# Convolution taps in turn over four channel blocks, and 89 of them beside the projections, in a hybrid encoder step on Trainium2

## The chip, the cores and the metric

One NeuronCore of one Trainium2 chip runs the whole layer as one program. The metric is the device time of that core in microseconds: the median of three runs, 654.04 us for the kernel before (653.13 to 656.37). Everything is float32 at the interface; there is one launch.

## The reference

One inference step of a one-layer streaming encoder over 528 prompt frames (16 learned meta tokens and 512 frames) and 32 sample frames of a running stream. Cut to what matters here:

```python
h = rmsnorm(x, g_mix)
proj = h @ w_in                                   # 1024 -> 2560
a_val, a_gate, q, k, v = jnp.split(proj, [512, 1024, 1536, 2048], axis=-1)
u = a_val * jax.nn.sigmoid(a_gate)                # 512 channels
u_hist = jnp.concatenate([conv_hist, u], axis=1)
a_out = jax.nn.silu(layernorm(causal_dwconv(u_hist, conv_w, conv_b), ln_g, ln_b))   # 31 taps per channel
b_out = head_rmsnorm(stick_breaking(q, k_all, v_all, q_start), g_sb)                # 8 heads x 64
x = x + jnp.concatenate([a_out, b_out], axis=-1) @ w_out
x = x + hier_moe(rmsnorm(x, g_ffn), ...)          # 32 experts, 2 per token
```

The depthwise convolution gives `conv[ch, t] = sum over j of w[j, ch] * u[ch, t + j]`, j = 0 to 30, and its result is needed first by the layer norm over channels. Outputs are both streams' final rows and the new keys, values and convolution histories.

## The kernel before

The five engines run their own instruction streams, joined by semaphores. The time falls into these stages: input norm and transposes (to about 50 us), the projections (to 153 us), attention (159 to 282 us), output projection and router (to about 390 us), the experts (to about 620 us) and the final norm.

**Projections.** TensorE computes the first 2048 columns of `w_in` as 16 products of 128 columns each, in the order gate 0, value 0, gate 1, value 1, ... (four channel blocks i), then k and q in four pairs. Each is done as high and low parts in fp32r: 3 x 16 matmuls of 288 columns, 48 in all (line 903). ScalarE rounds each weight tile to its high part (`upper`, line 1366), Pool subtracts it from the tile for the low part (`lower`, line 658: 128 x 1024, two SBUF inputs). `upper(j)` waits until product j - 3 is done. TensorE's product j waits for both parts, and from j = 4 to 11 also for the sigmoid (`sig_done`, even j) and for the gated product (`u_done`, odd j) of the pair four products before, since they share PSUM banks; there are eight banks, two for each product.

**The gated product.** For each channel block i VectorE waits for both projections and the sigmoid, and writes `u = value * sigmoid(gate)` with three instructions (lines 1609 to 1611, a PSUM and an SBUF input each).

**Taps.** The convolution of block i is 31 VectorE instructions over 128 x 590 (both streams with their histories lie side by side): the first is a `tensor_scalar` (line 1593), the others a `scalar_tensor_tensor` (line 1595) that multiplies a shifted slice of `u` with a weight per partition and adds the running `conv[:, i, :]`. `tap` passes each one to `link`, which makes the engine wait for its completion before the next instruction. After block i's last tap two instructions add the bias (line 1599) and give `yc_ready`. The list `taps` goes through block 0's 31 taps, then block 1's, and so on. `TAPS_EARLY = (13, 13, 13, 33)` of them, 72, follow the four gated products; the remaining 52 go into attention's steps, two each (`TAPS_STEP`).

```python
def link(ins):
    chain[0] += 1
    ins.then_inc(dve_chain, 1)
    dve.wait_ge(dve_chain, chain[0])
```

**Into attention.** TensorE transposes eight blocks of cached keys into PSUM (line 950, with a filler matmul at line 956 behind each). ScalarE copies the even ones to SBUF (line 1398), VectorE the odd ones (line 1677), which stand behind the 72nd tap in its program. Transpose n waits from n = 4 on for the copy of n - 4. The first scores wait for all eight copies.

**Attention.** 46 steps: 14 for the sample stream and the prompt's last frames (256 columns for all heads, "few") and 32 for the prompt (one head and one block of 128 keys, 128 to 512 columns, "many"); two few and one many take turns until the few are out at step 20. In step s TensorE makes scores (lines 966, 968 or 979, 982), ScalarE |z|, exp and ln (lines 1417, 1419, 1435), VectorE the softplus (`softplus`, line 1654), Pool the running sum of earlier blocks (lines 701 to 715), TensorE adds it to the scores (`reduce_later`, lines 996 to 1001), ScalarE exponentiates (line 1407) and TensorE weighs the values (`weigh`, lines 1014, 1028). In VectorE's program step s holds the softplus of step s - 1, two taps, and the output copy of a finished unit (lines 1665, 1670). From `LN_STEP = 30` the layer norm goes on between: Pool adds the four `yc` (line 685) in steps 27 to 29, TensorE takes the mean (line 1037) in step 30, VectorE the deviations from step 31.

**Behind attention** come the output projection (line 1098), stores, the router, and the experts, whose weights (2048 KB and 1024 KB for each expert) stream in behind one another. SyncE issues their first loads after the outputs of attention have been stored.

Of the kernel before, what the change touches and what calls it, by code (L numbers as in the profile page):

```python
# [11 lines left out]
ALU = mybir.AluOpType  # L12
# [12 lines left out]
NI = CC // P  # L25
# [8 lines left out]
TAPS = 31  # L34
HIST = TAPS - 1
UW = HIST + TP + HIST + TS
# [7 lines left out]
PAIRS = NE // 2  # L44
RING = 3
HALVED = 2
TAPS_EARLY = (13, 13, 13, 33)
TAPS_STEP = 2
LN_STEP = 30
LAG = 5  # L50
# [7 lines left out]
def build(nc, x_prompt, x_sample, cache_k, cache_v, cache_conv, meta, g_mix, w_in, conv_w, conv_b,  # L58
          ln_g, ln_b, g_sb, w_out, g_ffn, w_rg, b_rg, w_re, b_re, w_ei, w_eo, g_fin,
          y_p, y_s, nk_p, nv_p, ncv_p, nk_s, nv_s, ncv_s):  # L60
    with ExitStack() as ctx:
        def sb(name, shape, dt=F32):
            return ctx.enter_context(nc.sbuf_tensor(name, shape, dt))

        def sem(name):
            return ctx.enter_context(nc.semaphore(name))
# [24 lines left out]
        u = uflat.rearrange("p (i t) -> p i t", i=NI)  # L91
# [10 lines left out]
        cwt = sb("cwt", [P, NI, TAPS])  # L102
# [13 lines left out]
        def part(lo, n):  # L116
            return big[:, lo:lo + n]
# [4 lines left out]
        conv = part(14336, 4 * (UW - HIST)).rearrange("p (i t) -> p i t", i=NI)  # L122
# [123 lines left out]
        dve_chain = sem("dve_chain")  # L246
# [358 lines left out]
        def _(pool):  # L605
# [48 lines left out]
            def lower(j):  # L654

                slot = win[j % WSLOTS]
                pool.wait_ge(w_hi_ready, j + 1)
                pool.tensor_tensor(w_lo[j % WSLOTS], slot, w_hi[j % HSLOTS].bitcast(F32), ALU.subtract).then_inc(w_lo_ready, 1)  # L658
# [1 line left out]
            for j in range(13):  # L660
                lower(j)
            for i in range(NI):

                split = min(13 + 2 * i, 16)
                if i in (1, 2):
                    pool.wait_ge(qpair_ready, 2 * i + 1)
                    for j in range(11 + 2 * i, split):
                        lower(j)
                pool.wait_ge(w_lo_ready, split)
                pool.wait_ge(qk_done, 2 * i + 2)  # L670
                for r in range(2):
                    pool.tensor_copy(qpair[64 * r:64 * r + 64, :, i, 32 * r:32 * r + 32],
                                     qt[64 * r:64 * r + 64, i, 512:COLS].rearrange("p (a t) -> p a t", a=2)).then_inc(qpair_ready, 1)

            pool.wait_ge(z_ready, 1)
            for s, st in enumerate(steps):
# [3 lines left out]
                i = s - LN_STEP + NI  # L680
# [5 lines left out]
                i = s - LN_STEP - 3  # L686
# [842 lines left out]
        def _(dve):  # L1529
            chain = [0]  # L1530
# [5 lines left out]
# [5 lines that stand above are left out]
# [47 lines left out]
            low_part(4)  # L1588


            def tap(i, j):
                if j == 0:
                    link(dve.tensor_scalar(conv[:, i, :], u[:, i, 0:CW], cwt[:, i, 0:1], None, ALU.mult))
                else:
                    link(dve.scalar_tensor_tensor(conv[:, i, :], u[:, i, j:j + CW], cwt[:, i, j:j + 1],  # L1595
                                                  conv[:, i, :], ALU.mult, ALU.add))
                if j == TAPS - 1:
                    for dst, src in ((yc[:, i, 0:TP], conv[:, i, 0:TP]), (yc[:, i, S0:COLS], conv[:, i, US:US + TS])):
                        dve.tensor_scalar(dst, src, vt[:, 8 + i:9 + i], None, ALU.add).then_inc(yc_ready, 1)

            CW = UW - HIST
            taps = [(i, j) for i in range(NI) for j in range(TAPS)]
            dve.wait_ge(small_ready, 3)
            for i in range(NI):
                dve.wait_ge(proj_done, 2 * i + 2)
                dve.wait_ge(sig_done, i + 1)

                b, sg = proj_bank(2 * i + 1), sgm[i % 2]
                dve.tensor_tensor(u[:, i, HIST:HIST + HALF], ps[:, b, 0:HALF], sg[:, 0:HALF], ALU.mult).then_inc(conv_done, 1)
                dve.tensor_tensor(u[:, i, HIST + HALF:HIST + TP], ps[:, b + 1, 0:TP - HALF], sg[:, HALF:TP], ALU.mult).then_inc(conv_done, 1)  # L1610
                dve.tensor_tensor(u[:, i, UW - TS:UW], ps[:, b + 1, S0 - HALF:HALF], sg[:, S0:COLS], ALU.mult).then_inc(u_done, 1)
                dve.wait_ge(conv_done, 2 * i + 2)
                dve.wait_ge(u_done, i + 1)
                for _ in range(TAPS_EARLY[i]):
                    tap(*taps.pop(0))

            def deviation(i):

                if i == 0:
                    dve.wait_ge(mean_done, 1)  # L1620
                    dve.wait_ge(yc_ready, 2 * NI)
                dve.scalar_tensor_tensor(halves(yc[:, i, :]), ps[:, 6:8, 0:HALF], 1.0 / CC,
                                         halves(yc[:, i, :]), ALU.mult, ALU.add).then_inc(dev_ready, 1)

            def variances():
                dve.wait_ge(var_done, 1)
                dve.tensor_scalar(halves(lnv), ps[:, 6:8, 0:HALF], -1.0 / CC, EPS, ALU.mult, ALU.add).then_inc(lnv_ready, 1)

            def refine(j):

                if j == 0:
                    dve.wait_ge(lnr_done, 1)
                    dve.wait_ge(lnv_ready, 1)
                    link(dve.tensor_tensor(lnt, lnr, lnr, ALU.mult))
                elif j == 1:
                    link(dve.tensor_tensor(lnt, lnt, lnv, ALU.mult))
                elif j == 2:
                    link(dve.tensor_scalar(lnt, lnt, -0.5, 1.5, ALU.mult, ALU.add))
                else:
                    link(dve.tensor_tensor(lnr, lnr, lnt, ALU.mult))  # L1640
                    dve.wait_ge(dev_ready, NI)

            def normed(i):
                dve.tensor_tensor(yc[:, i, :], yc[:, i, :], lnr, ALU.mult).then_inc(norm_ready, 1)


            def softplus(s):
                st = steps[s]
                (r0, r1), n = st["rows"], st["n"]
                dve.wait_ge(l_done, s + 1)  # L1650
                if s >= 3:
                    dve.wait_ge(zr_ready, s - 2)
                    dve.wait_ge(cs_ready, sums[s - 3])
                dve.scalar_tensor_tensor(el[s % 3][r0:r1, 0:n], ps[r0:r1, s % 4, 0:n], 0.0, za[s % 3][r0:r1, 0:n],  # L1654
                                         ALU.max, ALU.add).then_inc(el_ready, 1)

            def unit_out(s):
                st = steps[s]
                if not st["last"]:
                    return  # L1660
                dve.wait_ge(av_done, s + 1)
                o = ps[:, unit_bank(st["unit"]), :]
                if "h" in st:
                    h = st["h"]
                    dve.tensor_copy(ot[:, 0:4, 64 * h:64 * h + 64],
                                    o[:, 0:256].rearrange("p (t d) -> p t d", t=4)).then_inc(o_ready, 1)
                else:
                    p0 = st["p0"]
                    for q in range(4):
                        ins = dve.tensor_copy(ot[p0:p0 + 32, 4, :].rearrange("p (a h d) -> p a h d", a=2, h=4)[:, :, q, :],  # L1670
                                              o[32 * q:32 * q + 32, 0:128].rearrange("p (a d) -> p a d", a=2))
                    ins.then_inc(o_ready, 1)
# [6 lines left out]
            for s in range(NS + 4):  # L1679
                if 0 <= s - LN_STEP - 1 < NI:  # L1680
                    deviation(s - LN_STEP - 1)
                if s == LN_STEP + 10:
                    variances()
                if 0 <= s - LN_STEP - 12 < 4:
                    refine(s - LN_STEP - 12)
                if 0 <= s - LN_STEP - 16 < NI:
                    normed(s - LN_STEP - 16)
                if 1 <= s <= NS:
                    softplus(s - 1)
                for _ in range(TAPS_STEP):  # L1690
                    if taps:
                        tap(*taps.pop(0))
                if s >= 4:
                    unit_out(s - 4)

# [2 lines left out]
            for lo, w, cc in ((0, P, slice(0, 4)), (0, 64, slice(4, 5))):  # L1698
# [6 lines left out]
                ins = dve.tensor_tensor(o4, o4, st8.unsqueeze(2).broadcast_to([w, k * HEADS, HD]), ALU.mult)  # L1705
# [289 lines left out]
```

## Time and profile before

| what | before |
|---|---|
| median of 3 runs | 654.04 us (653.13 to 656.37) |
| the profiled execution | 654.35 us, its span 652.6 us |
| mean granted clock of TensorE | 0.937 |
| TensorE (matmul) busy | 557.4 us, 85% of the span |
| VectorE busy | 297.4 us, 46% |
| ScalarE, Pool busy | 165.8 us, 163.0 us |
| DMA | 144.44 MB, mean 221 GB/s; 94% busy from 390 us on |

The span goes from the first to the last instruction; the execution's time has 1.75 us more around it. Matmuls overlap in the records, so TensorE's busy time is an upper reading. Durations of single instructions are in ns or us from start to the acknowledged end; where two of one engine overlap, the start-to-start time is what counts for its throughput. "Idle before" stands in square brackets with what ended it.

### The profile page before, as it was taken

How to read it: one execution, taken by the hardware profiler on the slowest of the kernel's cores; microseconds unless marked ns; L12 is line 12 of the kernel's file. 1: busy time of each engine (PE TensorE's matmuls, PEld its weight loads, DVE VectorE, ACT ScalarE, POOL GpSimd, SP SyncE). 2: the span in 40 equal slices, each digit the busy share in tenths (PEclk: the TensorE clock that was granted, in tenths of full speed). 3: DMA queues.
4: the chain of work that ended last, by engine and by line, in shares of the span. 5: the costliest groups of instructions: out<-in, count | busy, mean ns of one | idle time of the engine just before them, and what ended most of it. 6: DMA issues, size and time to landing. Idle time of an engine off the chain costs nothing.

```text
span 652.6 us, 8215 instructions
## 1 busy us (share of the span) xinstructions
PE 557.4 (85%) x3117; PEld 344.8 (53%) x3118; DVE 297.4 (46%) x483; ACT 165.8 (25%) x321; POOL 163.0 (25%) x215
## 2 busy tenths in 40 slices
PE   3999999999999989988999879999997877879700
PEld 2449999998777566645455473434332322323200
DVE  1531999998789823453415862121120210202037
ACT  2222122213466647732111210101010000000112
POOL 2041534441434444231100330121120210200013
PEclk9999999999599989988999969999998997989955
DMA  8703523105006000002974739999999999999675
GB/s 279 192 1 102 157 74 89 34 1 172 28 3 258 1 0 1 1 5 73 320 302 162 286 108 421 422 424 422 421 426 425 423 426 426 425 418 423 262 273 168
DMA packets 42747, 144.44 MB, mean 221 GB/s; under 512 B 6967, under 2 KB 23375, under 8 KB 34008
## 3 DMA queue, kind: packets, MB, share of 16 engines
q1 hardware_dynamic: 38103, 134.78, 53.1%
q0 software_dynamic: 4608, 9.18, 3.8%
q8 instruction: 22, 0.36, 0.2%
q14 instruction: 14, 0.11, 0.0%
HBM read 136.16 MB, written 15.39 MB: 232 GB/s over the span
## 4 chain that ended last, share of the span: by engine, by line
PE 44%; DVE 22%; DMA 20%; SPq 6%; issue 2%; POOL 2%; ACT 2%; DVEq 0%; POOLq 0%; ACTq 0%
DVE big L1595 16%; DMA low<-in_w_expert_in 11%; PE ps L1257 9%; PE ps L1098 7%; DMA big<-in_w_expert_out 4%; PE ps L874 4%; PE ps L1282 3%; SPq L567 3%; PE ps L1001 3%; SPq L524 2%; PE ps L966 2%; PE ps L903 2%; DMA big<-y_dram 2%; PE ps L1014 1%; PE ps L996 1%
## 5 line engine op out<-in xcount | busy, mean ns | idle before, releaser
L1595 DVE SCALAR_TENSOR_TENSOR big<-low,cwt,big 128x590 f32<-128x590 f32 x120 | 126.8, 1056 | 3.6
L1257 PE MATMUL ps<-big,cw 128*64 128x512 f32 x352 | 79.5, 603 | 12.8 <-DMA big<-in_w_expert_in 6.5
L1909 DVE TENSOR_TENSOR low<-low,ps 128x256 f32<-128x256 f32 x16 | 6.7, 421 | 181.1 <-ACT low L1492 181.1
L903 PE MATMUL ps<-cw_r 128*128 128x288 f32 x256 | 73.0, 295 | 0.0
L903 PE MATMUL ps<-low_r,cw_r 128*128 128x288 f32 x256 | 72.8, 294 | 0.0
L903 PE MATMUL ps<-cw_r,big_r 128*128 128x288 f32 x256 | 72.7, 294 | 0.0
L1257 PEld LDWEIGHTS ps<-big,cw 128*64 128x64 f32 x352 | 28.5, 139 | 62.0 <-issue 62.0
L1098 PE MATMUL ps<-cw,low 128*128 128x512 f32 x128 | 58.1, 610 | 1.7 <-ACT low L1440 1.2
L658 POOL TENSOR_TENSOR big_r<-big,cw_r 128x1024 fp32r<-128x1024 f32 x16 | 40.7, 2547 | 55.1 <-ACT cw_r L1366 55.1
L903 PEld LDWEIGHTS ps<-cw_r 128*128 128x128 f32 x256 | 47.4, 188 | 0.4 <-issue 0.4
L1282 PE MATMUL ps<-big,low 128*64 128x512 f32 x176 | 40.2, 597 | 8.3 <-DVE low L1915 7.3
L903 PEld LDWEIGHTS ps<-cw_r,big_r 128*128 128x128 f32 x256 | 47.2, 188 | 0.0
L903 PEld LDWEIGHTS ps<-low_r,cw_r 128*128 128x128 f32 x256 | 47.2, 187 | 0.0
L1257 PE MATMUL ps<-low 128*64 128x512 f32 x160 | 39.4, 649 | 7.5 <-DMA low<-in_w_expert_in 7.5
L1098 PEld LDWEIGHTS ps<-cw,low 128*128 128x128 f32 x128 | 24.4, 195 | 30.3 <-issue 29.2
L1500 ACT ACTIVATE cw<-ps,low 128x1024 f32<-128x1024 f32 x16 | 17.8, 1114 | 86.4 <-PE ps L1282 86.4
L1492 ACT ACTIVATE low<-ps 128x256 f32<-128x256 f32 x16 | 6.1, 383 | 126.2 <-PE ps L1257 126.2
L1654 DVE SCALAR_TENSOR_TENSOR big<-ps,big 128x256 f32<-128x256 f32 (+4 forms) x46 | 21.5, 470 | 34.2 <-ACT big L1435 29.1
L751 POOL CAST low<-low 128x1 int32<-128x1 f32 (+1 forms) x16 | 3.0, 189 | 130.1 <-PE ps L1241 118.3
L645 POOL TENSOR_TENSOR stat<-stat,nhalf 128x1 f32<-128x1 f32 (+1 forms) x15 | 16.0, 1068 | 78.0 <-DVE stat L1754 39.4
L1001 PE MATMUL ps<-big,negs 128*128 128x256 f32 (+4 forms) x92 | 33.7, 450 | 0.3 <-DVE big L1654 0.3
L1257 PEld LDWEIGHTS ps<-low 128*64 128x64 f32 x160 | 14.2, 151 | 32.1 <-issue 32.1
(247 smaller groups left out, 834.8 us busy)
## 6 DMA issues: line engine op xcount, KB each, us to landing
big<-in_w_expert_in SPq DMA_DIRECT2D x20, 2048.0 KB, 25.5
big<-in_w_expert_out SPq DMA_DIRECT2D x22, 1024.0 KB, 29.1
low<-in_w_expert_in SPq DMA_DIRECT2D x8, 2048.0 KB, 25.8
big<-in_w_in SPq DMA_DIRECT2D x20, 512.0 KB, 5.1
low<-in_w_expert_out SPq DMA_DIRECT2D x10, 1024.0 KB, 32.8
cw<-in_w_out SPq DMA_DIRECT2D x1, 4096.0 KB, 14.1
low<-in_w_expert_in SPq DMA_DIRECT2D x4, 1024.0 KB, 34.4
big<-in_w_expert_in SPq DMA_DIRECT2D x4, 1024.0 KB, 27.8
```

What stands on the lines that cost most here:

```text
L567: sp.dma_start(wi[q][:, ks], w_ei[0, 2 * g + half].rearrange("(p k) n -> p k n", p=P)[:, ks]).then_inc(landed[q], 16)
L645: pool.tensor_tensor(t, t, nhalf[0:t.shape[0], :].broadcast_to(list(t.shape)), ALU.pow).then_inc(rstd_ready, 1)
L658: pool.tensor_tensor(w_lo[j % WSLOTS], slot, w_hi[j % HSLOTS].bitcast(F32), ALU.subtract).then_inc(w_lo_ready, 1)
L874: mm = pe.matmul(ps[0:w, 4 + c % 2, :], ht[:, k, P * c:P * c + w], wv[:, k, :], start=k == 0, stop=k == KD - 1)
L903: return pe.matmul(ps[:, proj_bank(j) + half, 0:HALF], w[:, k, :], h[:, k, cols], start=first, stop=last, skip_group_check=True)
L1001: pe.matmul(z[r0:r1, 0:n], ntri[r0:r1, r0:r1], el[s % 3][r0:r1, 0:n], start=False, stop=True, skip_group_check=True).then_inc(zr_ready, 1)
L1098: mm = pe.matmul(ps[0:w, 4 + 2 * (c % 2) + n, :], mixt[:, k, P * c:P * c + w], wout[:, k, 512 * n:512 * n + 512], start=k == 0, stop=k == ...
L1257: mm = pe.matmul(ps[TILE * half:TILE * half + TILE, GU_BANK[s], :], xt[s][:, k, TILE * half:TILE * half + TILE], wi[2 * s + half][:, k, :] ...
L1282: mm = pe.matmul(ps[TILE * half:TILE * half + TILE, 4 + m, :], gact_t[:, k, TILE * half:TILE * half + TILE], wo[2 * s + half][:, k, 512 * ...
L1500: act.activation(yg[s].rearrange("p (m n) -> p m n", m=2), ps[:, 4:6, :], ACT.Copy, scale=gat[s]).then_inc(yg_ready, 1)
L1595: link(dve.scalar_tensor_tensor(conv[:, i, :], u[:, i, j:j + CW], cwt[:, i, j:j + 1], conv[:, i, :], ALU.mult, ALU.add))
L1654: dve.scalar_tensor_tensor(el[s % 3][r0:r1, 0:n], ps[r0:r1, s % 4, 0:n], 0.0, za[s % 3][r0:r1, 0:n], ALU.max, ALU.add).then_inc(el_ready, 1)
```

## The change

Taps are no longer taken from a list. `tap(units)` picks the channel block with the most taps left among those whose product is there, but not the block of the tap before (unless there is no other), and waits only for the last tap of the block that it picks, not for the one ahead. After a block's last tap the engine waits for that tap and adds the bias. `TAPS_EARLY` has nine entries: 10, 12, 12 and 8 taps follow the four products, and the sum of the other five, 47, follows at once over all four blocks; that makes 89 before the copies of the cached keys. Attention's steps call `tap(NI)` twice each as long as taps are left. Pool's low parts keep their place and order (the diff takes an empty line from them).

```diff
-TAPS_EARLY = (13, 13, 13, 33)
+TAPS_EARLY = (10, 12, 12, 8, 8, 8, 8, 8, 15)
...
             for i in range(NI):
-
                 split = min(13 + 2 * i, 16)
...
-            def tap(i, j):
+            CW = UW - HIST
+            taps_left, tapped, last_tap = [TAPS] * NI, [0] * NI, [None]
+
+            def tap(units):
+
+                others = [i for i in range(units) if taps_left[i] and i != last_tap[0]]
+                if not others and not taps_left[last_tap[0] or 0]:
+                    return
+                i = max(others, key=lambda i: taps_left[i]) if others else last_tap[0] or 0
+                j = TAPS - taps_left[i]
                 if j == 0:
-                    link(dve.tensor_scalar(conv[:, i, :], u[:, i, 0:CW], cwt[:, i, 0:1], None, ALU.mult))
+                    ins = dve.tensor_scalar(conv[:, i, :], u[:, i, 0:CW], cwt[:, i, 0:1], None, ALU.mult)
                 else:
-                    link(dve.scalar_tensor_tensor(conv[:, i, :], u[:, i, j:j + CW], cwt[:, i, j:j + 1],
-                                                  conv[:, i, :], ALU.mult, ALU.add))
+                    dve.wait_ge(dve_chain, tapped[i])
+                    ins = dve.scalar_tensor_tensor(conv[:, i, :], u[:, i, j:j + CW], cwt[:, i, j:j + 1],
+                                                   conv[:, i, :], ALU.mult, ALU.add)
+                chain[0] += 1
+                ins.then_inc(dve_chain, 1)
+                tapped[i], last_tap[0] = chain[0], i
+                taps_left[i] -= 1
                 if j == TAPS - 1:
+                    dve.wait_ge(dve_chain, tapped[i])
                     for dst, src in ((yc[:, i, 0:TP], conv[:, i, 0:TP]), (yc[:, i, S0:COLS], conv[:, i, US:US + TS])):
                         dve.tensor_scalar(dst, src, vt[:, 8 + i:9 + i], None, ALU.add).then_inc(yc_ready, 1)

-            CW = UW - HIST
-            taps = [(i, j) for i in range(NI) for j in range(TAPS)]
             dve.wait_ge(small_ready, 3)
+            early = list(TAPS_EARLY)
             for i in range(NI):
...
-                for _ in range(TAPS_EARLY[i]):
-                    tap(*taps.pop(0))
+                for _ in range(early.pop(0)):
+                    tap(i + 1)
+            for _ in range(sum(early)):
+                tap(NI)
...
                 for _ in range(TAPS_STEP):
-                    if taps:
-                        tap(*taps.pop(0))
+                    tap(NI)
```

## Rows read from the trace of the kernel before

**Rows 1.** The page's chain that ended last, shares by line.
```profile
DVE big L1595 16%; DMA low<-in_w_expert_in 11%; PE ps L1257 9%; PE ps L1098 7%; DMA big<-in_w_expert_out 4%; PE ps L874 4%; PE ps L1282 3%; SPq L567 3%; PE ps L1001 3%; SPq L524 2%; PE ps L966 2%; PE ps L903 2%; DMA big<-y_dram 2%; PE ps L1014 1%; PE ps L996 1%
```

**Rows 2.** VectorE's timeline, 64 to 160 us: start, us, then the instructions merged.
```profile
64.48 0.46 DVE L1609 TENSOR_TENSOR low<-ps,big 128x288 f32<-128x288 f32 x1 [12.19 <-PE ps L903]
...
66.02 16.46 DVE L1595 SCALAR_TENSOR_TENSOR big<-low,cwt,big 128x590 f32<-128x590 f32 x12
...
119.88 0.46 DVE L1609 TENSOR_TENSOR low<-ps,big 128x288 f32<-128x288 f32 x1
...
146.89 0.65 DVE L1599 TENSOR_SCALAR big<-big,vt 128x528 f32<-128x528 f32 x2
...
148.00 7.79 DVE L1595 SCALAR_TENSOR_TENSOR big<-low,cwt,big 128x590 f32<-128x590 f32 x9
155.83 1.29 DVE L1677 COPY cw<-ps 128x512 f32<-128x512 f32 x2
```

**Rows 3.** Stretches: length; PE, PEld, DVE, ACT, POOL busy (count); clock, DMA, GB/s.
```profile
64.40:155.80 91.40, 91.40 (x699) 91.40 (x699) 88.36 (x88) 21.22 (x26) 35.89 (x20) 1.00 0.24 70
...
159.20:192.60 33.40, 32.07 (x259) 23.96 (x260) 27.82 (x41) 19.02 (x51) 13.44 (x14) 0.80 0.16 57
192.60:207.60 15.00, 14.47 (x153) 10.85 (x154) 14.03 (x24) 9.75 (x28) 5.75 (x7) 1.00 0.52 195
207.60:225.40 17.80, 17.18 (x106) 10.56 (x104) 17.20 (x30) 11.80 (x30) 8.13 (x9) 1.00 0.18 73
...
248.40:257.10 8.70, 8.70 (x45) 5.70 (x45) 2.30 (x5) 7.28 (x19) 6.09 (x8) 1.00 0.01 2
...
164.00:178.00 14.00, 13.40 (x85) 10.03 (x86) 10.65 (x16) 5.87 (x17) 5.73 (x6) 0.51 0.03 11
```

**Rows 4.** Timeline of TensorE at the hand-over to attention.
```profile
156.57 0.66 PE L950 MATMUL ps<-ident,big 128*128 128x128 f32 x4 [0.43 <-DVE cw L1677]
...
159.49 0.61 PE L979 MATMUL ps<-big,low 128*32 128x64 f32 x8 [0.72 <-issue]
```

**Rows 5.** VectorE's waits from 192 to 226 us, and its timeline there.
```profile
DVE big L1654 <- ACT big L1435: 0.5, 1, 0.5
...
192.69 0.42 DVE L1654 SCALAR_TENSOR_TENSOR big<-ps,big 128x256 f32<-128x256 f32 x1
193.03 1.69 DVE L1595 SCALAR_TENSOR_TENSOR big<-low,cwt,big 128x590 f32<-128x590 f32 x2
...
225.36 0.87 DVE L1654 SCALAR_TENSOR_TENSOR big<-ps,big 128x512 f32<-128x512 f32 x2
```

**Rows 6.** Durations (ns: min/median/max) of taps and of line 1644, and 1644's timeline.
```profile
L1595 DVE SCALAR_TENSOR_TENSOR big<-low,cwt,big x9: 832/833/836, 148.0 to 155.0; 128x590 f32<-128x590 f32 x9
...
L1644 DVE TENSOR_TENSOR big<-big x3: 748/750/751, 277.9 to 279.2; 128x576 f32<-128x576 f32 x3
...
277.88 2.09 DVE L1644 TENSOR_TENSOR big<-big 128x576 f32<-128x576 f32 x3
...
L1595 DVE SCALAR_TENSOR_TENSOR big<-low,cwt,big x1: 823/823/823, 166.7 to 166.7; 128x590 f32<-128x590 f32 x1
```

**Rows 7.** A tap that meets Pool (chain), and two of Pool's subtractions (timeline).
```profile
73.25 2.86 DVE big L1595
...
90.95 2.93 POOL L658 TENSOR_TENSOR big_r<-big,cw_r 128x1024 fp32r<-128x1024 f32 x1 [3.44 <-ACT cw_r L1366]
...
110.43 2.41 POOL L658 TENSOR_TENSOR big_r<-big,cw_r 128x1024 fp32r<-128x1024 f32 x1 [4.41 <-ACT cw_r L1366]
```

**Rows 8.** TensorE's timeline: scores of 384 columns, four steps apart, with and without taps.
```profile
217.42 0.91 PE L966 MATMUL ps<-low 64*128 64x384 f32 x2
...
228.40 0.91 PE L966 MATMUL ps<-low 64*128 64x384 f32 x2
...
242.31 0.91 PE L966 MATMUL ps<-low 64*128 64x384 f32 x2
...
251.58 0.91 PE L966 MATMUL ps<-low 64*128 64x384 f32 x2
```

## The prediction

> **What bounds the kernel now.** I read the page first, its chain of work that ended last: the depthwise convolution's tap (line 1595) alone has 16% of it, more than any other line [rows 1]. A tap is one VectorE instruction over 590 columns, and `link` makes the next one wait for it. Next comes VectorE's timeline in the projections: after the first product, at 64.5, the engine does taps until 155.8 us with only the short product groups and block ends between them, and then copies its four quarters of the cached keys, for which attention waits [rows 2]. The table of busy times says that TensorE is busy in all 91.4 us of this stretch too, at the full clock [rows 3]: the taps don't slow the projections. They matter at the hand-over only. TensorE waits 0.43 us for VectorE's first copy at 156.57, and its first attention matmul starts at 159.49 [rows 4], 3.66 us after VectorE came free.
>
> In attention each of the first 26 steps has a softplus on VectorE (line 1654) and two taps. From step 12 to 26 VectorE waits for ScalarE once, for 0.5 us [rows 5], and it looks like the bound. But the table shows TensorE busy in 14.47 of 15.00 and 17.18 of 17.80 us of these steps, and in 32.07 of 33.40 before them [rows 3]. Two engines are full here, so relief for VectorE can give back little more than TensorE's gaps.
>
> **What a tap costs, with and without the wait.** Nine taps in a row on one block take 7.79 us at 833 ns each: one starts every 0.870 us [rows 2, 6]. An instruction that waits for nothing starts before the one ahead has ended: three of line 1644, 750 ns each, take 2.09 us, a start every 0.670, which is 80 ns early [rows 6]. A softplus (192.69, 0.42 long) has a tap behind it at 193.03, also 80 early, and such a tap took 823 ns [rows 5, 6]. For a tap behind a tap of another block I take 0.823 - 0.081 = 0.742 us, 0.128 less than now. Bounds: 0.685 (line 1644's start-to-start with 14 columns more, as if the factor per partition cost nothing) and 0.870.
>
> **The Pool toll.** A low-part subtraction of Pool (2.41 us) that meets a tap makes it 2.86 us instead of 0.84; where it finds a tap in progress it lasts up to 2.93, since it waits first [rows 7]. So a meeting costs VectorE 2.02 us in a stream that pauses between taps anyway, and 2.14 in one whose pause is 0.128 shorter; bounds 2.02 and 2.41. Twelve subtractions fall into the tap stretch and they stay. What lies beside the product group (0.98 us from its start to the first tap), which reads PSUM and one tile only, is free.
>
> **The sum for the projections.** The order follows from the diff: ten taps of block 0, nine of which wait as now; then 12, 12 and 8 + 47 that always change block, three first ones and 76 others, whose waits are long satisfied. That is 89 before the copies for 72 now, and no block's last one is among them. TensorE needs 699 matmuls in 91.4 us, 6.3 us for the 48 of a projection [rows 3], so pairs are through at 64.4, 77.0, 89.6 and 102.2; subtractions come each 6.5 us: 90.95 and 110.43 are the first and last of four [rows 7].
> - Block 0: 66.0 + 9 x 0.870 + 2 x 2.02 = 77.9 (now 82.5).
> - Block 1: group 0.98, then Pool (78.3 to 80.6) in the way for 1.65; first tap 0.44, 11 x 0.742 = 8.16, one meeting 2.14: 91.3.
> - Block 2: 0.98, the rest of Pool's 90.95 one 1.15, 0.44, 8.16, 2.14: 104.1.
> - Block 3: 0.98, 1.15, 0.44, 54 x 0.742 = 40.07, five meetings 10.7, 0.2 for small Pool copies: 157.7.
> VectorE comes to the copies 1.9 us later than now (155.8), with 17 more taps done. The fourth product moves from 119.9 [rows 2] to 104.1, so the sigmoid and the projections that wait for products lose nothing. With the cheap tap it would be 153.4, which gains no more than TensorE's 0.43; the dear meetings would add 2.
>
> **The sum for attention.** 35 taps are left instead of 52: steps 0 to 17 carry them, 18 to 25 none. A step of 256 columns takes VectorE 0.34 + 0.86 + 0.87 now and 0.34 + 2 x 0.742 = 1.82 after. It is worth what TensorE's gaps are [rows 3]: of the first stretch's 1.33 us I take 0.5 (the rest fills the pipeline, and stays); of 0.53 + 0.62 in the next two 0.8. Around step 25 more stands still: from the scores at 217.42 to those at 228.40 are 10.98 us, while the same four steps without taps take 9.27 (242.31 to 251.58) [rows 8]. Of these 1.71 I take 1.5, the rest being in the gaps above. Against it, the four blocks now end in steps 15 to 17: four times the bias pair (0.65 us [rows 2]), less one tap, 1.9 us in three steps. A softplus isn't needed by TensorE at once in a step that TensorE fills, so I take 0.4 of it as uncovered (bounds 0 and 1.9). The layer norm's mean has its fixed place at step 30. Relief: 0.5 + 0.8 + 1.5 - 0.4 = 2.4 us, bounds 0 and 4.2 (1.33 + 0.53 + 0.62 + 1.71).
>
> TensorE's clock is at 1.2 of 2.4 GHz from 164 to 178, behind the thin start of attention [rows 3]. A later start lengthens the gap ahead of it by 1.9 us; the slow stretch may come earlier or last longer. I price that at 0, bounds -1 and +2. All loads of expert weights are issued behind attention's outputs, so the shift is carried to the end one to one.
>
> **Total:** +1.9 - 2.4 = -0.5 us against the profiled execution's own 654.35, so 653.85; the median of the runs stands 0.31 below that execution, so 653.5. About 0.5% (3.3 us) is what a measurement here can tell from no change.
>
> **Rivals.**
> 1. *VectorE alone bounds steps 12 to 25.* For it: no idle time there. Against it: TensorE's 97%. Then these 13 steps, 32.67 us now (192.69 to 225.36) [rows 5], go down to the pace of four steps without taps that fill the stretch of 8.70 us [rows 3], 28.3 in all: -4.4, with the 0.5 from before -4.9; so 654.04 + 1.9 - 4.9 = 651.0, and with the cheap tap 649.1. Chance 0.25.
> 2. *The later hand-over isn't paid back.* TensorE's gaps give 0.5, the bunched block ends cost their 1.9, the copies come 1.9 later: 657.3. For it: two full engines. Chance 0.13.
> 3. *Leaving the wait out doesn't shorten the stream.* Place: the 76 taps. They keep 0.870, so the copies come at 167.4, 11.6 behind now, while TensorE idles; attention gets 1.3 back: 664.3. Against it are the pairs above, all 80 ns early. It decides over the forecast from a start-to-start of some 0.78 us, where 76 x 0.04 adds 3. Chance 0.07.
> The Trainium skill speaks for this rival: "VectorE: DVE Perf Modes", section on the DRAIN you can't avoid, states that eight copies took 13.88 us with a semaphore after each and after the last alone. By that rule the time would be 664.3; this trace disagrees in its own pairs [rows 6].
> 4. *Pool is shut out.* Between taps that wait there is a pause in which Pool gets in; a stream without waits may leave it none. Place: the 55 taps behind the last product. If subtractions wait for its end (105.1 + 40.5 = 145.6), projection 11 starts at 148.0 and not at 64.4 + 9 x 6.3 = 121.1; that is 26.9, less 0.4 (the copies aren't waited for) and 2.4: 678. It decides from where a subtraction issued at 110.43 is held for over 8 us. Against it: Pool gets in after one tap in each meeting now [rows 7]. Chance 0.05.
> The skill's "SBUF — State Buffer", section on who interferes with whom, states that a VectorE instruction with two SBUF inputs and a Pool one that reads SBUF block each other whole. The tap of 2.86 us agrees; no row shows Pool against two taps that don't wait.
>
> **How the numbers follow.** The forecast has 0.50, its own range is 651 to 656.5. Faster by over 0.5% is below 650.8: two thirds of rival 1 and a tail of the forecast, 0.25. Slower by over 0.5% is above 657.3: rivals 3 and 4, half of 2, and a little for the clock, 0.20. Within: 0.55. The range for 8 in 10 takes in most of rivals 1 and 2 and leaves out 3, 4 and the lowest end: 649.5 to 658.
>
> **What would show it.** A start-to-start of the taps near 0.742 from 105 to 157, with meetings of about 2.9 us; product groups at 64.5, 77.9, 91.3 and 104.1; line 1677's first copy at 157.7 and the first attention matmul at 161.3; no taps after step 17; TensorE without gaps in steps 18 to 27. It would be wrong if the first copy came before 155.5 or after 160, if TensorE paused in the projections, or if VectorE, taps gone, ran steps 18 to 25 at under 2.2 us each.

## Result and the profile after

The changed kernel takes 668.44 us (median of 4 runs, 661.47 to 677.59) against 655.20 us for the kernel before beside it: a ratio of 1.0168 with a 95% interval of 1.0126 to 1.0211. It is slower by 1.7%; forecast was 653.5 us, no change. Run once more later, it gave 666.70 us and 1.0189 (1.0127 to 1.0251). The ratios leave out disturbed runs of either kernel. The profiled execution (661.47 us, span 659.7) is the fastest of the four, so it shows the loss at its smallest.

The first view is VectorE's timeline in the projections, as in [rows 2]. Line 1604 is the tap now, 1601 a block's first one, 1613 the bias, 1692 the copy of cached keys, 1669 the softplus.

```profile
63.75 0.46 DVE L1622 TENSOR_TENSOR low<-ps,big 128x288 f32<-128x288 f32 x1 [12.19 <-PE ps L902]
...
77.04 0.45 DVE L1622 TENSOR_TENSOR low<-ps,big 128x288 f32<-128x288 f32 x1
...
90.54 0.45 DVE L1622 TENSOR_TENSOR low<-ps,big 128x288 f32<-128x288 f32 x1
...
103.46 0.44 DVE L1622 TENSOR_TENSOR low<-ps,big 128x288 f32<-128x288 f32 x1
...
106.05 51.00 DVE L1604 SCALAR_TENSOR_TENSOR big<-low,cwt,big 128x590 f32<-128x590 f32 x54
156.97 1.27 DVE L1692 COPY cw<-ps 128x512 f32<-128x512 f32 x2
```

This trace stands 0.7 us earlier than that of before as a whole (63.75 for 64.48). With that added, the product groups come at 77.8, 91.3 and 104.2 and the copies at 157.7: to 0.1 us what the sum said (77.9, 91.3, 104.1, 157.7). The 54 taps that follow block 3's first one take 51.00 us; summed were 40.07 + 10.7 + 0.2. The change does what it says. Five of Pool's subtractions fall among these taps, as counted; two of them:

```profile
109.71 2.41 POOL L658 TENSOR_TENSOR big_r<-big,cw_r 128x1024 fp32r<-128x1024 f32 x1 [3.91 <-ACT cw_r L1365]
...
122.45 2.90 POOL L658 TENSOR_TENSOR big_r<-big,cw_r 128x1024 fp32r<-128x1024 f32 x1 [2.24 <-ACT cw_r L1365]
```

Pool is not shut out: its subtractions last 2.4 to 2.9 us between taps that don't wait, as they did between those that do [rows 7].

Next TensorE's timeline, at the hand-over (as [rows 4]) and around step 16's `reduce_later` (line 998):

```profile
157.70 0.66 PE L949 MATMUL ps<-ident,big 128*128 128x128 f32 x4 [2.28 <-DVE cw L1692]
...
160.62 0.61 PE L978 MATMUL ps<-big,low 128*32 128x64 f32 x8 [0.72 <-issue]
...
203.98 1.06 PE L978 MATMUL ps<-big,low 128*128 128x64 f32 x8
206.94 0.70 PE L998 MATMUL ps<-big,negs 128*128 128x256 f32 x2 [1.90 <-DVE big L1669]
...
208.95 1.97 PE L978 MATMUL ps<-big,low 128*128 128x64 f32 x8
```

The hand-over is as forecast too. What stands out is the gap of 1.90 us ahead of 206.94, where TensorE waits for the softplus of step 16, and the matmuls behind it: the eight matmuls of a step's scores take 1.06 us ahead of the gap and 1.97 us behind it. The kernel before has a gap in the same place, of 0.53 us:

```profile
203.67 0.70 PE L999 MATMUL ps<-big,negs 128*128 128x256 f32 x2 [0.53 <-DVE big L1654]
```

What kept the softplus is in VectorE's timeline:

```profile
199.10 1.59 DVE L1604 SCALAR_TENSOR_TENSOR big<-low,cwt,big 128x590 f32<-128x590 f32 x2
200.72 0.65 DVE L1613 TENSOR_SCALAR big<-big,vt 128x528 f32<-128x528 f32 x2
201.28 0.42 DVE L1680 COPY big<-ps 128x256 f32<-128x256 f32 x1
201.62 0.42 DVE L1669 SCALAR_TENSOR_TENSOR big<-ps,big 128x256 f32<-128x256 f32 x1
201.95 0.82 DVE L1604 SCALAR_TENSOR_TENSOR big<-low,cwt,big 128x590 f32<-128x590 f32 x1
202.81 0.99 DVE L1613 TENSOR_SCALAR big<-big,vt 128x528 f32<-128x528 f32 x2
203.72 0.82 DVE L1604 SCALAR_TENSOR_TENSOR big<-low,cwt,big 128x590 f32<-128x590 f32 x1
204.57 0.64 DVE L1613 TENSOR_SCALAR big<-big,vt 128x528 f32<-128x528 f32 x2
205.25 1.18 DVE L1685 COPY big<-ps 32x128 f32<-32x128 f32 x4
206.46 0.42 DVE L1669 SCALAR_TENSOR_TENSOR big<-ps,big 128x256 f32<-128x256 f32 x1
```

Between two softplus (201.62 and 206.46) lie 4.84 us: two taps, two blocks' bias pairs, one of them 0.99 us long beside an instruction of Pool, and the output copy of a finished unit, four instructions in 1.18 us. In the kernel before the same two softplus were 3.62 us apart, with the same output copy between them but no bias pair, since no block ended there:

```profile
199.57 0.41 DVE L1654 SCALAR_TENSOR_TENSOR big<-ps,big 128x256 f32<-128x256 f32 x1
199.90 2.04 DVE L1595 SCALAR_TENSOR_TENSOR big<-low,cwt,big 128x590 f32<-128x590 f32 x2
201.97 1.19 DVE L1670 COPY big<-ps 32x128 f32<-32x128 f32 x4
203.19 0.42 DVE L1654 SCALAR_TENSOR_TENSOR big<-ps,big 128x256 f32<-128x256 f32 x1
```

Last the table of stretches (columns as in [rows 3]), the changed kernel and, under it, the kernel before in the same four:

```profile
162.00:181.00 19.00, 18.80 (x112) 14.27 (x111) 14.06 (x21) 9.01 (x26) 7.08 (x8) 0.55 0.09 35
181.00:200.00 19.00, 19.00 (x181) 13.68 (x179) 16.02 (x25) 12.59 (x33) 6.69 (x9) 1.00 0.01 2
200.00:208.00 8.00, 6.10 (x65) 4.73 (x63) 7.75 (x18) 4.67 (x14) 2.23 (x3) 0.97 0.78 286
208.00:226.00 18.00, 18.00 (x107) 10.84 (x106) 3.41 (x9) 7.38 (x18) 2.56 (x6) 0.54 0.27 107
```

```profile
162.00:181.00 19.00, 18.05 (x125) 13.16 (x126) 15.39 (x23) 9.13 (x28) 7.32 (x8) 0.64 0.13 50
...
200.00:208.00 8.00, 7.47 (x84) 5.48 (x83) 7.72 (x13) 5.49 (x16) 4.18 (x4) 1.00 0.98 380
208.00:226.00 18.00, 16.78 (x105) 10.56 (x104) 17.43 (x30) 12.15 (x30) 7.78 (x8) 1.00 0.16 64
```

The clock's column is the one to read. The granted clock has two levels, 1.2 and 2.4 GHz, so a mean of 0.54 over 18 us is (1 - 0.54) x 2 x 18 = 16.6 us at the lower one. A run of time at the lower level is called a slow stretch here. The changed kernel has two long ones in attention: 17.1 us from 163 on (before: 13.7 us) and 17.1 us from 207.6 on (before: none). In the second TensorE is 100% busy and VectorE works 3.41 us of 18: a full engine at half speed, and VectorE isn't what it waits for. Attention ends where VectorE squares its output, in the changed kernel and, under it, in the kernel before:

```profile
291.06 2.29 DVE L1714 TENSOR_TENSOR big<-big 128x2048 f32<-128x2048 f32 x1
```

```profile
282.07 2.29 DVE L1700 TENSOR_TENSOR big<-big 128x2048 f32<-128x2048 f32 x1
```

With the 0.7 us offset that is 9.7 us later, 1.9 of them from the later start and 7.8 from an attention (first scores to this line) of 130.4 us (160.62 to 291.06) for 122.6 (159.49 to 282.07).

### The profile page after: what moved, and what is told of

Same layout as the page of the kernel before. It is cut to its first block, busy times and chain, and to the rows that moved or that the text cites. A ratio compares the mean times of both kernels' runs of the same rounds, so it can differ in the third digit from the quotient of the medians.

```text
span 659.7 us, 8189 instructions
## 1 busy us (share of the span) xinstructions
PE 564.3 (86%) x3117; PEld 349.7 (53%) x3118; DVE 287.7 (44%) x483; ACT 166.3 (25%) x321; POOL 159.8 (24%) x215
## 4 chain that ended last, share of the span: by engine, by line
PE 50%; DMA 19%; DVE 18%; SPq 6%; issue 2%; ACT 2%; POOL 2%; DVEq 0%; POOLq 0%; ACTq 0%
DVE big L1604 13%; DMA low<-in_w_expert_in 11%; PE ps L1256 9%; PE ps L1097 8%; DMA big<-in_w_expert_out 4%; PE ps L873 4%; PE ps L1000 4%; PE ps L965 3%; PE ps L1281 3%; SPq L567 3%; SPq L524 2%; PE ps L902 2%; PE ps L978 2%; PE ps L1013 2%; DMA big<-y_dram 2%
## 5 line engine op out<-in xcount | busy, mean ns | idle before, releaser
L1604 DVE SCALAR_TENSOR_TENSOR big<-low,cwt,big 128x590 f32<-128x590 f32 x120 | 113.2, 1001 | 0.4
L1256 PE MATMUL ps<-big,cw 128*64 128x512 f32 x352 | 82.5, 622 | 15.0 <-DMA big<-in_w_expert_in 6.8
L1097 PE MATMUL ps<-cw,low 128*128 128x512 f32 x128 | 56.4, 595 | 1.7 <-ACT low L1439 1.2
L1256 PE MATMUL ps<-low 128*64 128x512 f32 x160 | 36.7, 612 | 5.1 <-DMA low<-in_w_expert_in 5.1
L1000 PE MATMUL ps<-big,negs 128*128 128x256 f32 (+4 forms) x92 | 36.4, 483 | 0.2 <-DVE big L1669 0.2
L750 POOL CAST low<-low 128x1 int32<-128x1 f32 (+1 forms) x16 | 3.0, 189 | 126.2 <-PE ps L1240 114.4
L873 PE MATMUL ps<-big,low 128*128 128x512 f32 x64 | 29.1, 608 | 0.0
```

Of the source, the lines that this page charges most:

```text
L873: mm = pe.matmul(ps[0:w, 4 + c % 2, :], ht[:, k, P * c:P * c + w], wv[:, k, :], start=k == 0, stop=k == KD - 1)
L1000: pe.matmul(z[r0:r1, 0:n], ntri[r0:r1, r0:r1], el[s % 3][r0:r1, 0:n], start=False, stop=True, skip_group_check=True).then_inc(zr_ready, 1)
L1097: mm = pe.matmul(ps[0:w, 4 + 2 * (c % 2) + n, :], mixt[:, k, P * c:P * c + w], wout[:, k, 512 * n:512 * n + 512], start=k == 0, stop=k == ...
L1256: mm = pe.matmul(ps[TILE * half:TILE * half + TILE, GU_BANK[s], :], xt[s][:, k, TILE * half:TILE * half + TILE], wi[2 * s + half][:, k, :] ...
L1604: ins = dve.scalar_tensor_tensor(conv[:, i, :], u[:, i, j:j + CW], cwt[:, i, j:j + 1], conv[:, i, :], ALU.mult, ALU.add)
```

## Experiments

Theory A: the ends of the four blocks, bunched in steps 15 to 17, leave TensorE idle for 1.9 us, its clock falls behind that, and in a stage that TensorE fills the low clock makes the time longer. Rival B: the longer wait ahead of attention (2.28 us for 0.43) and its first slow stretch are the cost. Rival C: taps that don't wait disturb attention wherever they are.

**The bias pairs moved out of steps 15 to 17.**

```diff
                 if j == TAPS - 1:
-                    dve.wait_ge(dve_chain, tapped[i])
-                    for dst, src in (...):
-                        dve.tensor_scalar(dst, src, vt[:, 8 + i:9 + i], None, ALU.add).then_inc(yc_ready, 1)
...
                 for _ in range(TAPS_STEP):
                     tap(NI)
+                if 18 <= s < 18 + NI:
+                    bias(s - 18)
```

> The changed kernel, but the four pairs of bias instructions are taken out of steps 15 to 17 and stand one each in steps 18 to 21, where no taps are left. Theory A (the ends of the four blocks, bunched, leave TensorE idle for 1.9 us at 205 us, its clock then falls to 1.2 GHz for 17 us in a stage that TensorE fills): the gap goes, no half-clock stretch around 208 to 225, 8 us less than the changed kernel's 661.5, so 652 to 654. Rival B (the later start of attention, TensorE idle 2.3 us at 155, is what costs, through the first half-clock stretch of 17 us): the time stays over 659. Rival C (taps that don't wait disturb something in attention, whatever their place): stays over 659 too, with TensorE's gaps spread.

Measured: ratio 1.0121 (1.0019 to 1.0222), 659.48 to 670.13 us, the profiled execution 659.48. The gap and the second slow stretch are gone:

```profile
208.44 0.70 PE L998 MATMUL ps<-big,negs 128*128 128x256 f32 x2 [0.24 <-DVE big L1670]
```

```profile
162.00:181.00 19.00, 18.80 (x111) 14.62 (x111) 14.52 (x21) 9.08 (x26) 7.21 (x8) 0.54 0.09 34
181.00:200.00 19.00, 19.00 (x159) 12.89 (x159) 12.60 (x19) 11.08 (x28) 4.68 (x5) 0.83 0.01 2
200.00:208.00 8.00, 8.00 (x83) 6.68 (x82) 7.52 (x15) 5.50 (x17) 2.93 (x4) 1.00 0.34 117
208.00:226.00 18.00, 17.76 (x142) 11.35 (x141) 9.10 (x23) 11.77 (x30) 4.93 (x10) 1.00 0.45 182
```

Attention lasts 124.1 us, 6.3 less. But the time is not the 652 to 654 expected. The first slow stretch is 24 us long here ((1 - 0.54) x 2 x 19 + (1 - 0.83) x 2 x 19), though up to step 15 this program is the changed kernel's, which had 17; so that stretch varies from execution to execution. It doesn't explain the time, however: the kernel with a filler in step 18, below, has the same 24 us and a ratio of 1.0016. The profiles of the two differ behind attention, with 372.9 and 367.8 us from its end to the last instruction. What keeps this kernel at 1.0121 (from four runs) stays open.

**The kernel before with VectorE held up in step 16.**

```diff
+                if s == 16:
+                    for _ in range(3):
+                        link(dve.tensor_copy(osq[:, 0, :], osq[:, 1, :]))
                 if s >= 4:
                     unit_out(s - 4)
```

> The kernel before, with VectorE held up in step 16 alone by three extra waited copies of 128 x 512 (about 1.4 us). Theory A: TensorE's gap of 0.53 us at 203 grows to about 1.9, its clock falls to 1.2 GHz behind it, and the time rises by 6 to 9 us, far beyond the 1.4 put in. Rivals B and C: no more than 1.4 us, 654 to 656.

Measured: 663.15 us, ratio 1.0080 (1.0043 to 1.0117); in its profile attention lasts 129.9 us for 122.6, so 7.3 more for 1.4 put in.

```profile
204.28 1.22 PE L999 MATMUL ps<-big,negs 128*128 128x256 f32 x2 [1.91 <-DVE big L1654]
```

```profile
200.00:208.00 8.00, 6.09 (x43) 4.70 (x41) 7.68 (x14) 3.28 (x10) 2.97 (x4) 0.77 1.00 403
208.00:226.00 18.00, 18.00 (x96) 10.77 (x96) 11.84 (x20) 8.40 (x20) 4.01 (x5) 0.63 0.12 46
```

The kernel before, with its taps in their old order and their old waits, gets the same gap and the same slow stretch, 3.7 + 13.3 = 17.0 us. So the new order of taps isn't needed for it: rival C falls, and A is shown from the other side.

**One copy in place of three** (`range(1)`), to see whether any delay there does it.

> The kernel before with one extra waited copy (about 0.47 us) in step 16 in place of three. TensorE's gap there grows from 0.53 to about 1.0 us. If a gap of this size is enough for the low clock, a second half-clock stretch of about 17 us follows and the time is as with three copies, 661 to 664. If it isn't: 0.5 us over the kernel before at most.

Measured: 654.46 us, ratio 1.0015 (0.9976 to 1.0055). TensorE's gap is 0.99 us, and no slow stretch follows, so not every delay there does it; the stretch at the start of attention has 10.3 us.

**Fillers on TensorE in place of a change on VectorE.** The changed kernel, step 18's scores made three times, which puts about 1.8 us of work (24 matmuls in 2.84 us for 8 in 1.06) where TensorE waited:

```diff
-                for i in range(NI):
+                for i in [i for _ in range(3 if s == 18 else 1) for i in range(NI)]:
```

> The changed kernel, but TensorE makes the scores of step 18 three times over (1.9 us more work, just ahead of its 1.9 us gap, same result). VectorE's program is untouched. Theory A: no half-clock stretch behind it, so 652 to 655. If it is VectorE's lateness in steps 15 to 17 as such, and not the clock, the time stays at 661 or more. Rival B: stays over 659.

Measured: 655.85 us (653.95 to 663.45), ratio 1.0016 (0.9969 to 1.0063).

```profile
200.00:208.00 8.00, 8.00 (x95) 6.47 (x84) 7.10 (x14) 5.63 (x17) 2.93 (x4) 1.00 0.27 91
208.00:226.00 18.00, 17.88 (x155) 12.40 (x153) 8.33 (x22) 10.70 (x28) 4.37 (x9) 1.00 0.48 194
```

This is the plainest of the runs: VectorE's program is the changed kernel's to the last instruction, its bunched block ends included, TensorE has more to do, and no loss is left that can be told from no change. The lateness of VectorE as such was worth little. Rival B falls as the account of the 1.7% (a few tenths of a per cent would not show): TensorE still waits 2.27 us ahead of attention here, and the first slow stretch has 24 us.

**The order of the change with the old waits.** A wait on the tap ahead is put back into `tap`.

```diff
                 ins.then_inc(dve_chain, 1)
+                dve.wait_ge(dve_chain, chain[0])
```

> The changed kernel's order of taps, but each tap waits for the one ahead, as in the kernel before. The tap then starts every 0.87 us and not every 0.74; 76 x 0.128 = 9.7 us more ahead of the copies of the cached keys, which start at about 166.7 (157.0 in the changed kernel). TensorE idle about 12 us ahead of attention. Time about 10 us over the changed kernel's if the clock does the same, 668 to 674.

Measured: 680.81 us, ratio 1.0345 (1.0241 to 1.0450), from two runs.

```profile
159.28 7.78 DVE L1604 SCALAR_TENSOR_TENSOR big<-low,cwt,big 128x590 f32<-128x590 f32 x9
167.09 1.29 DVE L1693 COPY cw<-ps 128x512 f32<-128x512 f32 x2
```

The copies start at 167.09 for 156.97: 10.1 us for 76 waits, 0.13 each, with the nine taps at 7.78 us as in [rows 2]. The overlap of independent taps is real and shortens VectorE's stream beside the projections by 10 us. TensorE waits 13.04 us ahead of attention here, and at step 16 its gap is 2.45 us; behind that comes a slow stretch of 13.7 us, behind the start of attention one of 24.

**Fewer early taps and later bias pairs.** 86 taps ahead of the copies (the last entry of `TAPS_EARLY` is 12), one bias pair each in steps 20 to 23.

> The changed kernel with 86 taps ahead of the copies of the cached keys (12 in place of 15 in the last entry), 38 taps in steps 0 to 18, and the four bias pairs one each in steps 20 to 23. The copies start at 154.7 and TensorE no longer waits for them. Theory A+B (both the bunched ends and the late hand-over cost, each through TensorE's clock): one half-clock stretch in attention, of about 14 us as in the kernel before, attention over by 281, time 651 to 654. If the first half-clock stretch is long for another reason than the idle time ahead of it: it stays at 17 to 24 us, and the time at 655 to 658.

Measured: 657.36 us, ratio 1.0039 (0.9996 to 1.0082). TensorE waits for nothing at the hand-over, as intended, and 0.24 us at most later; the second slow stretch is gone. The first isn't: in the profiled execution it is 41 us long, by far the longest seen; that execution took 664.35 us, one of the longest of its ten (652.36 to 665.96), so the others may well have less. The wait at the hand-over doesn't set its length alone.

**Fillers at the start of attention**, in three kernels. Two more of the filler matmuls of line 956 behind transposition 4, counted from 0 (ten in the changed kernel, which waits longer there), three behind the last, and the scores of step 3 twice:

```diff
-                pe.matmul(ps[:, 4, 0:P], ident[:, :], ident[:, :], start=True, stop=True, skip_group_check=True)
+                for _ in range(3 if n == 4 else 4 if n == 7 else 1):
+                    pe.matmul(ps[:, 4, 0:P], ident[:, :], ident[:, :], start=True, stop=True, skip_group_check=True)
...
-                for i in range(NI):
+                for i in [i for _ in range(2 if s == 3 else 1) for i in range(NI)]:
```

With the 86 early taps:

> As the kernel with 86 early taps and late bias pairs, and TensorE has filler work at the start of attention: 2 more filler matmuls behind the fourth transposition and 3 behind the last, and the scores of step 3 made twice (about 2.5 us of work in places where it waits). If the low clock at 164 us follows from TensorE's idle time at 155 to 164, it goes or gets short: attention 4 to 7 us shorter, time 646 to 650. If not: no change from the kernel without fillers.

Measured: 650.14 us (647.40 to 657.80), ratio 0.9950 (0.9915 to 0.9984).

```profile
162.00:181.00 19.00, 18.88 (x196) 14.46 (x196) 18.97 (x27) 13.17 (x37) 10.39 (x11) 1.00 0.14 51
181.00:200.00 19.00, 18.76 (x199) 14.04 (x187) 18.75 (x31) 12.64 (x34) 8.24 (x9) 1.00 0.32 111
...
208.00:226.00 18.00, 17.11 (x92) 11.07 (x84) 5.83 (x17) 12.47 (x32) 7.28 (x13) 1.00 0.00 1
```

No slow stretch in attention up to 226 us; it lasts 114.4 us (159.37 to 273.74), 8.2 less than before. It is the one kernel of the study that is faster than both, by 0.5%.

In the kernel before:

> The kernel before with the same filler work at the start of attention and nothing else. If the low clock at 164 us follows from TensorE's idle time ahead of it: the stretch of 13.7 us goes, time 3 to 6 us below the kernel before. If not: 0 to 2 us above it.

Measured: ratio 1.0111 (1.0002 to 1.0221) from four runs of 652.79 to 664.68 us, a miss: the slow stretch is 13.7 us as without fillers, attention 122.7 us.

In the changed kernel, with step 18's filler:

> The changed kernel, VectorE untouched, with fillers in all three places where TensorE waits: 10 more filler matmuls behind the fourth transposition (where it waits 2.3 us), 3 behind the last, scores of step 3 twice and of step 18 three times. Clock theory for both stretches: neither comes, time 648 to 652. Clock theory for the second alone: as the kernel with the filler at step 18 only, 655.

Measured: 652.47 us, ratio 0.9991 (0.9939 to 1.0043). No slow stretch between 162 and 226 in its profile, attention 117.9 us for 130.4.

In the changed kernel, without step 18's:

> The changed kernel with fillers at the start of attention alone (10 more behind the fourth transposition, 3 behind the last, scores of step 3 twice), and none at step 18. Clock theory: the first half-clock stretch is gone, and the second, behind TensorE's 1.9 us gap of steps 15 to 17, stays with about 17 us; attention lasts 8 to 9 us longer than with the third filler (118.2), 127, and the time is 659 to 663. If one filler at the start cures both: 650 to 655.

Measured: 665.48 us, ratio 1.0142 (1.0055 to 1.0229).

```profile
208.61 0.88 PE L999 MATMUL ps<-big,negs 128*128 128x256 f32 x2 [1.91 <-DVE big L1670]
```

```profile
162.00:181.00 19.00, 18.80 (x113) 14.62 (x112) 13.13 (x19) 9.09 (x26) 6.34 (x8) 0.57 0.13 50
...
208.00:226.00 18.00, 17.39 (x88) 11.00 (x89) 4.68 (x10) 6.70 (x16) 3.58 (x6) 0.53 0.36 145
```

The second stretch is there, 17 us long, behind the gap of 1.91, as theory A says. The first is there too, though up to step 17 this is the program of the kernel with all fillers, which had none (on another chip of the same kind; no run here tells whether the chip has a part in it). So the fillers at the start make full clock possible, not certain.

**The changed kernel once more.**

> The changed kernel as it is, once more beside the others. Clock theory: two half-clock stretches in attention again, the second of 17 us behind a 1.9 us gap near 205; the first of 17 to 24 us. Time 661 to 670.

Measured: 666.70 us, ratio 1.0189 (1.0127 to 1.0251). The gap is 1.91 us at 210.7, the first stretch 27 us (means of 0.57 and 0.71 in the first two stretches of the table), the second 17 ((1 - 0.63) x 2 x 18 up to 226 us and (1 - 0.90) x 2 x 18 in the next 18).

**The kernel before with a later start of attention** (four waited copies of 128 x 512 ahead of line 1677).

> The kernel before with four extra waited copies of 128 x 512 on VectorE (about 1.9 us) ahead of the copies of the cached keys, so that attention starts as late as in the changed kernel, with the taps as they were. If the length of the first half-clock stretch (10 to 14 us in the kernel before and its variants, 17 and more in the changed kernel's order) follows from TensorE's longer wait ahead of attention: 17 to 27 us here, and 3.5 to 8 us over the kernel before. If it follows from what the taps do in attention's first steps: 10 to 14 us, and about 1.9 us over.

Measured: four runs from 654.03 to 667.44 us, median 662.16 for 653.97, too scattered for an interval. The first stretch is 17.1 us, and attention ends at 285.17, 3.1 us later than in [rows 3]'s execution. The stretch is what the first expectation said, at its lower end; two of the four times (654.03 and 656.89) are near the second's and two (667.4) above both. It settles nothing.

| kernel | gap of TensorE at step 16 | first slow stretch | second |
|---|---|---|---|
| before | 0.53 | 13.7 | none |
| before, 1 copy in step 16 | 0.99 | 10.3 | none |
| before, 3 copies in step 16 | 1.91 | 13.7 | 17.0 |
| before, fillers at the start | 0.53 | 13.7 | none |
| before, late start | 0.53 | 17.1 | none |
| changed | 1.90 | 17.1 | 17.1 |
| changed, again | 1.91 | 27 | 17 |
| changed, fillers at the start | 1.91 | 17.1 | 17 |
| changed order, old waits | 2.45 | 24 | 13.7 |
| changed, filler in step 18 | none | 24 | none |
| changed, bias pairs late | 0.24 | 24 | none |
| changed, all fillers | none | none | none |
| 86 early, bias pairs late | 0.24 | 41 | none |
| 86 early, bias late, fillers | 0.24 | none | none |

All in us. Each trace also has a later gap of 1.8 us, in step 30, where TensorE waits for Pool's sums ahead of the layer norm's mean. It shows that a gap's length isn't all that counts: behind it the clock was low for some 3 us in ten of the fourteen traces, for 7 in three and not at all in one, the kernel before with one copy:

```profile
233.72 1.21 PE L1037 MATMUL ps<-big,negs 128*128 128x288 f32 x4 [1.80 <-POOL big L685]
```

```profile
226.00:244.00 18.00, 16.20 (x84) 10.83 (x82) 6.19 (x12) 10.79 (x26) 7.60 (x13) 1.00 0.00 0
```

Why 1.9 us at step 16 is followed by 17 us and 1.8 us at step 30 by so much less, no run here shows.

## Why the prediction was wrong

**Right:** the price of a tap without a wait (0.742 us), the meetings with Pool, each product group, the copies (157.7) and the first attention matmul (161.3 by before's scale); that the projections would not notice. Rival 3 said that leaving the waits out gains nothing and put the copies at 167.4. They came at 157.0 without the waits and at 167.1 with them put back, each in its own trace, so it is refuted. With it falls, for taps of this kind, what the Trainium skill ("VectorE: DVE Perf Modes", the DRAIN you can't avoid) found with eight copies, that a semaphore after each costs nothing. Rival 4 (Pool shut out) did not come.

**The step that failed** is the price of the bunched block ends, in two terms: "I take 0.4 of it as uncovered (bounds 0 and 1.9)" and, for TensorE's clock, "I price that at 0, bounds -1 and +2". The place was named rightly: 1.9 us of extra VectorE work in steps 15 to 17. Its cover was overrated. The output copy of a finished unit (1.19 us before, 1.18 now) falls into the same steps; it is no new work, but it had used up the cover, as the gap of 0.53 us there before shows, and the forecast's count of a step leaves it out. The gap went to 1.90, 1.4 us more. Above all the clock was priced for the start of attention alone, and the bunched ends only by the time that they leave uncovered. What they cost is mostly the clock behind the gap: 17 us at 1.2 GHz of an engine that has no idle time. That the stage is full was read correctly [rows 3], and it was used only as a lid on the gain, not as what makes each slow microsecond count.

How much is a slow microsecond worth? The changed kernel with fillers at the start alone has 34 us of them in its two long stretches and an attention of 131.5 us; with all fillers it has none and 117.9, with a gap of 1.9 us filled by about as much work. So 13.6 / 34 = 0.40 us for each. (With the short slow stretches of step 30 counted, 3 us in the one and 7 in the other, the price is 13.6 / 31 = 0.44. Two more pairs of traces give 0.35, the kernel before with and without three copies, and 0.50, the two executions of the changed kernel.) For the second stretch that is 6.8 us, for the 3.4 us that the first one is longer 1.4, and the gap adds 1.0 beyond the 0.4 in the forecast: 9.2, where attention's end stands 9.7 - (-0.5) = 10.2 us behind the forecast. That is an estimate from one execution of each, but it leaves little over. In the profiled execution some 2 us come back behind attention (368.6 us from its end to the last instruction, 370.5 before); that stretch took 367.8 to 375.8 us in the fourteen profiles, so this need not be the change's doing.

**The relief for attention** was about right in size, as far as can be told. The 86-tap kernel with fillers, at full clock, needs 114.4 us; before, 122.6 less 0.40 x 13.7 is 117.1. The difference is 2.7 us, 2.4 were forecast. With 0.35 and 0.50 in place of 0.40 it is 3.4 and 1.4, and the 86-tap kernel differs in its fillers and bias pairs too, so that the agreement is in part luck. In the changed kernel the relief can't be seen, because the clock takes more than that.

**Rival 2** had the sign and the steps (bunched ends, later copies), but as plain delays, 657.3 us. It had a chance of 0.13.

**What stays open** is the first slow stretch. It was 10 to 14 us in four profiles of the kernel before and its variants, 17 in one with a late start, and 17 to 41 in seven with the new order of taps, with two more that had none. Programs that are the same up to there gave 17, 24 and 27 us. Whether the order of the taps lengthens it, or the later start, or both, wasn't separated. Nor is it shown what it costs the changed kernel: the kernel with late bias pairs and the one with a filler in step 18 both have 24 us of it and no second one, and their ratios are 1.0121 and 1.0016.

## What to carry to other kernels

When work is moved off a step, look at where its end goes: things that used to end one by one may now end together, and on the engine that feeds a full TensorE even 2 us of lateness in one place can be followed by 17 us at half the clock, which cost some 7 us here (an estimate). Price a delay ahead of a TensorE-bound stage by the granted clock in the profile, not by its length, and read that column first when the time rises and no engine is idle. Independent VectorE instructions between dependent ones are worth 0.13 us each here, which is a gain only if TensorE is kept at work in the seams; here 1.8 us of filler matmuls in one seam took the ratio from 1.0168 to 1.0016.

## What the runs showed of the hardware

- A single gap of 1.9 us in TensorE's work at step 16, at full clock and behind 19 us without idle time, was followed by 17 us at 1.2 GHz in each of the four profiled executions that had it (two of the changed kernel, one with fillers at its start, one of the kernel before with three copies), whichever cause the gap had. One of 2.45 us in the same place was followed by 13.7 us, one of 0.99 by none.
- The length of a gap doesn't set the slow time alone: one of 1.8 us at step 30 was followed by some 3 us in ten traces, 7 in three and none in one.
- The clock can stay low while the engine is busy all the time: 19.00 of 19.00 us busy at a mean of 0.50 in the kernel with 86 early taps. A microsecond at the lower level cost 0.35 to 0.50 us of time in this stage (estimates from three pairs of traces).
- Executions whose programs are the same up to a point had first slow stretches of different length ahead of it (17, 24 and 27 us; none and 17).
- A tap that waits for nothing starts 80 ns before the end of the one ahead, a factor per partition included: 54 of them with five of Pool's subtractions took 51.00 us.
- A tap that meets one of these subtractions takes up to 2.98 us for 0.82, which agrees with the Trainium skill's "SBUF — State Buffer", section on who interferes with whom: a VectorE instruction with two SBUF inputs contends with one of Pool that reads SBUF, and the one that has the shared ports keeps them for the whole instruction. In the stream of taps that don't wait Pool got in each time: the five subtractions took 2.41 to 2.90 us.
